# GpSimd instead of VectorE computes the low weight half of one chunk in front of each of four layer norms

## The chip, the cores and the metric

The kernel runs on one core of a Trainium2 chip. The metric is device time in microseconds of one execution; lower is better. Engines are called PE (TensorE, with its weight loads as PEld), DVE (VectorE), ACT (ScalarE), POOL (GpSimd) and SP (SyncE).

## What is computed

A stack of four transformer-like layers on 256 tokens of width 1024, in float32. The part that matters here is the first two layers, each with two residual steps that end in a layer norm:

```python
def layer_norm(x, g, b):
    mu = jnp.mean(xf, axis=-1, keepdims=True)
    var = jnp.mean(jnp.square(xf - mu), axis=-1, keepdims=True)
    y = (xf - mu) * lax.rsqrt(var + LN_EPS) * g + b
...
for i in range(DEPTH):                      # DEPTH = 2
    mix = s5_mixer(h, ...) if i % 2 == 0 else stick_breaking_mixer(h, ...)
    h = layer_norm(ALPHA * h + mix, ln_mix_g[i], ln_mix_b[i])
    h = layer_norm(ALPHA * h + swiglu_ffn(h, w_gu[i], w_down[i]), ln_ffn_g[i], ln_ffn_b[i])
```

Behind them come two hybrid layers (attention, mLSTM, feed-forward) with RMS norms, which the change does not touch.

## The kernel before

**Weights in chunks.** All matrix products run as one sequence of weight chunks of 128 x 2048 float32 elements (1 MB), numbered through all layers. A chunk `c` lives in slot `c % 3` of three buffers: `raw` (as loaded), `w_hi` and `w_lo`. SP loads `raw` (two transfers of 512 KB, `load_chunk`, L390). ACT rounds it to a high part (`split_hi`, L395, counts `hi_done`). DVE computes the low part `w_lo = raw - w_hi` (`split_lo`, L400, counts `lo_done`). PE then makes three products of 128x128 weights with 128x256 activations for each of a chunk's 16 blocks: high by high (L419), high by low (L420), low by high (L421), or two wider ones (L429, L430) in some matrices. Both counts are plain counters of chunks: `lo_done >= c + 1` means that chunks 0 to `c` are split (`weights_split`), and so chunks must be counted in order. SP waits for `lo_done >= j - 2` before it loads chunk `j` into its slot.

**Look-ahead of three.** When PE has finished chunk `i`, ACT and DVE split chunk `i + 3` into the slot that has come free. In the matrices whose results are added to the residual (`evac == "resid"`) this is done by `resid_hi` on ACT (it waits for `chunk_done` of the chunk) and `resid_lo` on DVE.

**Order around a layer norm.** Every engine's order is written out by hand. There are four layer norms, n = 0 to 3, behind the matrices `ssm_out` (4 chunks), `down0` (11), `sb_out` (4) and `down1` (11). DVE's list for such a matrix is `resid_vector`: it adds the product tiles to the residual, prepares centred tiles `xn` and their squares, and calls `resid_lo` for the chunks. With 4 chunks the last two `resid_lo` (indices 2 and 3) stand together in front of the layer norm; with 11 chunks index 10 stands there. Then comes `layer_norm_vector`:

- L1124: the variance, from a PSUM row and `rstd` in SBUF. It waits for ACT's square and copy of the mean (`norm_scale`, L886 and L887). ACT then takes logarithm and exponential (L891, L894) to give `rstd`.
- `centre(q)` (L1129: `xn - dm_sb`) and `scale(q)` (L1134: `xn * rstd`) for four pairs of tiles; each has both inputs in SBUF. `centre` is followed by a wait of DVE for itself.
- ACT makes the normed tiles `res` and, for the first half, `x_hi` (`normed_pair`, L919, L928, L897); DVE makes `x_lo` (`low`, L1150, or L1119 for n = 3) and the second half of `x_hi`.
- `split(0)`, `split(1)`: DVE's `w_lo` of the next two chunks, whose `w_hi` ACT makes behind its normed tiles (`early_columns`).
- `normalised`, `early_gated`: corrections of the two early chunks, see next.

**What PE does meanwhile.** Behind the last residual chunk PE multiplies the first two chunks of the next matrix with the not yet normed values (`early_tensor`); the mean and scale are corrected afterwards by DVE (L1162, L1168) and ACT (L949, L953). These two chunks are 96 products. Then PE needs `x_lo` of the normed values (`xl_done`, pair by pair in its first chunk) and, for this third chunk, its weights: its number is `c = g.c0 + g.n - 1 + 3`, where `g` is the residual matrix. It is the chunk whose `w_lo` DVE computes last in front of the layer norm. For n = 1 and n = 3 the next users of the corrected early chunks are PE's attention scores (L1324) and the product at L2363.

**POOL.** GpSimd works only at the start (`s5_pool`, L2042 to L2113): tables for the state-space mixer, and the `w_lo` of chunk 0 (L2113), the same operation as L400.

Of the kernel before, what the change touches and what calls it, by code (L numbers as in the profile page):

```python
# [15 lines left out]
F32 = mybir.dt.float32  # L16
# [4 lines left out]
ALU = mybir.AluOpType  # L21
# [11 lines left out]
RING = 3  # L33
# [106 lines left out]
RESIDS = ("ssm_out", "down0", "sb_out", "down1", None, "out0", "ff2_0", "out1", "ff2_1")  # L140
# [106 lines left out]
def stack(nc, w, out):  # L247

    gemms, n_chunks = plan(w)
    G = {g.name: g for g in gemms}  # L250
    ctx = ExitStack()
    with ctx:
# [19 lines left out]
        raw = [sb(f"raw{s}", [P, CH], "raw", 4 * CH * s) for s in range(RING)]  # L272
# [63 lines left out]
        hi_done, lo_done = S("hi_done"), S("lo_done")  # L336
# [60 lines left out]
        def split_lo(dve, c, idx, k):  # L397
            s = (c + k) % RING
            dve.wait_ge(hi_done, idx + (c + 1))
            nc.vector.tensor_tensor(w_lo[s][:, :], raw[s][:, :], w_hi[s][:, :].bitcast(F32), ALU.subtract).then_inc(lo_done, 1)  # L400
# [357 lines left out]
        def early_chunks(n):  # L758

            return {0: ((G["gu0"], 0), (G["gu0"], 1)), 1: ((G["q0"], 0), (G["k0"], 0)), 2: ((G["gu1"], 0), (G["gu1"], 1)),  # L760
                    3: ((G["kv_0"], 0), (G["qa0_0"], 0))}[n]

        def x_index(n):

            return n + 1 if n < 3 else n
# [356 lines left out]
        def layer_norm_vector(dve, g, n):  # L1122
            dve.wait_ge(rstd_done, 3 * n + 2)
            nc.vector.tensor_tensor(rstd[:, :], PS[:, 3, T:2 * T], rstd[:, :], ALU.subtract).then_inc(v_done, 1)  # L1124
            twice = [t[:, :].unsqueeze(1).to_broadcast([P, 2, T]) for t in (dm_sb, rstd)]

            def centre(q):
                pair = xn[:, 2 * q:2 * q + 2, :]
                nc.vector.tensor_tensor(pair, pair, twice[0], ALU.subtract).then_inc(dve_step, 1)  # L1129
                dve.wait_ge(dve_step, v_count.one())  # L1130

            def scale(q):
                pair = xn[:, 2 * q:2 * q + 2, :]
                nc.vector.tensor_tensor(pair, pair, twice[1], ALU.mult).then_inc(scaled, 1)  # L1134

            def high(q):
                dve.wait_ge(res_normed, KT * n + 2 * q + 2)
                if n == 3:
                    for t in (2 * q, 2 * q + 1):
                        nc.vector.tensor_scalar(x_hi[:, t, :], res[:, t, :], gain(4, t), None, ALU.mult).then_inc(xh_done, 1)  # L1140
                    return
                nc.vector.tensor_copy(x_hi[:, 2 * q:2 * q + 2, :], res[:, 2 * q:2 * q + 2, :]).then_inc(xh_done, 2)

            def low(q):
                if n == 3:
                    gained_lo(dve, 4, 2 * q)
                    gained_lo(dve, 4, 2 * q + 1)
                    return
                dve.wait_ge(xh_done, KT * x_index(n) + 2 * q + 2)
                nc.vector.tensor_tensor(x_lo[:, 2 * q:2 * q + 2, :], res[:, 2 * q:2 * q + 2, :],  # L1150
                                        x_hi[:, 2 * q:2 * q + 2, :].bitcast(F32), ALU.subtract).then_inc(xl_done, 2)

            def split(slot):
                e, idx = early_chunks(n)[slot]
                split_lo(dve, e.c0 + RING, idx, idx)

            def normalised(slot):

                e, idx = early_chunks(n)[slot]
                dve.wait_ge(cols_copied, 2 * n + slot + 1)  # L1160
                for m in range(2):
                    ins = nc.vector.scalar_tensor_tensor(out=early[:, slot, m * T:(m + 1) * T], in0=dm_sb[:, :],  # L1162
                                                         scalar=col_sums[:, 2 * slot + m, 0:1],
                                                         in1=early_banks(slot)[:, m, 0:T], op0=ALU.mult, op1=ALU.add)
                ins.then_inc(dve_step, 1)
                dve.wait_ge(dve_step, v_count.one())
                both = early[:, slot, :].rearrange("p (a t) -> p a t", a=2)
                nc.vector.tensor_tensor(both, both, twice[1], ALU.mult).then_inc(early_done, 1)  # L1168

            centre(0)  # L1170
            dve.wait_ge(rstd_done, 3 * n + 3)
            scale(0)
            for q in range(1, 3):
                centre(q)
                scale(q)
            low(0)
            centre(3)
            scale(3)
            low(1)
            high(2)  # L1180
            low(2)
            high(3)
            low(3)
            split(0)
            split(1)
            if n == 3:
                square_sums(dve, 4, 0, 4)
            normalised(0)
            normalised(1)
            if n in (0, 2):  # L1190
                early_gated(dve, n, 0)
                early_gated(dve, n, 1)

        def early_gated(dve, n, slot):
            g, idx = early_chunks(n)[slot]
            z = idx + g.gated0 + 1
            dve.wait_ge(sig_done, z)
            dve.wait_ge(hid_done, idx + g.hid0)
            nc.vector.scalar_tensor_tensor(out=prod[:, 0:T], in0=early[:, slot, 0:T], scalar=col_sums[:, 2 * slot, 1:2],
                                           in1=early[:, slot, T:2 * T], op0=ALU.add, op1=ALU.mult).then_inc(z_done, 1)  # L1200
            dve.wait_ge(z_done, z)
            nc.vector.tensor_copy(hid_hi[:, idx, :], prod[:, 0:T]).then_inc(gated_hi, 1)
            dve.wait_ge(gated_hi, z)
            nc.vector.tensor_tensor(hid_lo[:, idx, :], prod[:, 0:T], hid_hi[:, idx, :].bitcast(F32),
                                    ALU.subtract).then_inc(hid_done, 1)
# [35 lines left out]
        def resid_vector(dve, g, n):  # L1241
            last = g.n - 1
            held = 2 if g.shape == "kt8" else last
            if g.half:
                half_vector(dve, g, n)
                return
            raw_columns(dve, n)
            if n == 3:
                gate_weights(dve)
            for idx in range(g.n):  # L1250
                for t in range(KT):
                    if g.ends[t][0] != idx:
                        continue
                    if n < 4 and t == 4:
                        shifted_tiles(dve, g, n)
                    if n < 4 and t >= 4:
                        shifted_tile(dve, g, n, t)
                    else:
                        add_tile(dve, g, t)
                    if n < 4 and t == 3:  # L1260
                        dve.wait_ge(resid_done, g.resid0 + 4)
                        shift_sum(dve, n)
                        raw_columns_lo(dve, g, n)
                    if n < 4 and t == 5:
                        pair_shift(dve, n)
                    if n in (1, 3) and t == 7:
                        fold_mean(dve, n, 7)
                    if n < 4 and t >= 4:
                        raw_tile_lo(dve, n, 2 * t - 8)
                        raw_tile_lo(dve, n, 2 * t - 7)  # L1270
                    if n == 6:
                        gained_lo(dve, n, t)
                        if t == 5:
                            square_sums(dve, n, 0, 2)
                        if t == 7:
                            square_sums(dve, n, 2, 4)
                    if n < 4 and t == 5:
                        add_squares(dve, n, 0)
                    if n < 4 and t == 6:
                        square_sums(dve, n, 1, 3)  # L1280
                        fold_mean(dve, n, 6)
                    if n in (0, 2) and t == 7:
                        fold_square(dve, n, 6)
                    if n in (1, 3) and t == 7:
                        fold_square(dve, n, 6)
                        fold_square(dve, n, 7)
                if n >= 4 or idx < held:
                    resid_lo(dve, g, idx)
            if n < 4:
                for idx in range(held, g.n):  # L1290
                    resid_lo(dve, g, idx)
            if n < 4:
                layer_norm_vector(dve, g, n)
# [1769 lines left out]
        @block.gpsimd  # L3063
        def _(pool):
            s5_pool(pool)

        @block.tensor
        def _(pe):
# [73 lines left out]
```

## Time and profile before

| | |
|---|---|
| median of 3 runs | 1345.09 us (1344.32 to 1345.76) |
| the profiled execution's own time | 1345.14 us |
| its span in the profile | 1343.3 us |
| granted clock of TensorE | 1.0 |
| PE busy, PEld busy | 98%, 93% of the span |
| DVE, ACT, POOL busy | 70%, 50%, 4% |
| `w_lo` on DVE (L400) | 207 instructions, 2.29 us each |
| `w_hi` on ACT (L395) | 207 instructions, 1.9 us each |
| a load of 512 KB, from issue to landing | median 4.5 to 5.1 us by tensor (5.1 for `ffn_w_gu`) |

PE is busy nearly all the time, but its loads and products overlap, so its share says little about small gaps. A stall shows in the starts of the weight loads instead: in a stretch without stalls they follow each other every 0.12 us.

### The profile page before, as it was taken

The page shows a single profiled execution, that of the slowest core. Times are in us where ns is not written, and L with a number is a line of the kernel's source. Part 1 is how long each engine was busy: PE and PEld are TensorE (multiplying, and loading weights), DVE is VectorE, ACT ScalarE, POOL GpSimd, SP SyncE. Part 2 cuts the span into 40 slices and gives each one's busy share as a digit, 9 for nine tenths or more (in the row PEclk, how much of TensorE's full clock was granted, in tenths as well). Part 3 has the DMA queues.
Part 4 walks back from the last instruction along what each step waited for, and adds up shares of the span by engine and source line. Part 5 has one row for each costly group of instructions (what it writes and reads, how often), then busy time and mean ns, then how long its engine had stood idle before and what let it go on. Part 6 is the DMA issues. An engine that isn't in the chain of part 4 may idle for free.

```text
span 1343.3 us, 25869 instructions
## 1 busy us (share of the span) xinstructions
PE 1314.0 (98%) x10699; PEld 1245.2 (93%) x10699; DVE 944.0 (70%) x1340; ACT 676.2 (50%) x838; POOL 56.7 (4%) x31
## 2 busy tenths in 40 slices
PE   5899999999999999999999999999999999999999
PEld 4599999988999999998989999998898999999988
DVE  8966976657865986657897788775457867877542
ACT  5774643334765653344666545444445554544332
POOL 6910000000000000000000000000000000000000
PEclk9999999999999999999999999999999999999999
DMA  8676486675443576666444456567664535556662
GB/s 157 158 185 185 133 221 184 188 190 180 145 148 96 157 208 185 187 188 176 153 137 147 155 159 217 189 184 192 188 188 127 157 123 192 189 188 187 188 188 63
DMA packets 342809, 227.81 MB, mean 170 GB/s; under 512 B 22616, under 2 KB 337792, under 8 KB 342592
## 3 DMA queue, kind: packets, MB, share of 16 engines
q1 hardware_dynamic: 341200, 226.33, 58.5%
q8 instruction: 67, 1.10, 0.3%
q10 hardware_dynamic: 1520, 0.20, 0.1%
q14 instruction: 22, 0.18, 0.0%
HBM read 224.40 MB, written 1.05 MB: 168 GB/s over the span
## 4 chain that ended last, share of the span: by engine, by line
PE 86%; DVE 7%; ACT 4%; issue 1%; POOL 1%; SPq 0%; DMA 0%; DVEq 0%; ACTq 0%; POOLq 0%
PE PS L419 20%; PE PS L420 20%; PE PS L421 20%; PE PS L429 12%; PE PS L430 6%; DVE w_lo L400 2%; ACT w_hi L395 1%; PE PS L1340 1%; DVE xn L1134 1%; DVE xn L1129 1%; DMA c_rows<-in_ssm_c_re_dram 0%; PE PS L1742 0%; PE PS L2430 0%; PE PS L1324 0%; DVE raw_lo L1089 0%
## 5 line engine op out<-in xcount | busy, mean ns | idle before, releaser
L400 DVE TENSOR_TENSOR w_lo<-raw,w_hi 128x2048 fp32r<-128x2048 f32 x207 | 473.6, 2291 | 144.1 <-ACT w_hi L395 143.3
L419 PE MATMUL PS<-x_hi,w_hi 128*128 128x256 f32 x1792 | 504.1, 281 | 1.0 <-DVE w_lo L400 0.5
L420 PE MATMUL PS<-x_lo,w_hi 128*128 128x256 f32 x1792 | 503.7, 281 | 0.0
L421 PE MATMUL PS<-x_hi,w_lo 128*128 128x256 f32 x1792 | 503.3, 281 | 0.0
L395 ACT ACTIVATE w_hi<-raw 128x2048 fp32r<-128x2048 f32 x207 | 396.4, 1915 | 203.2 <-PE PS L430 139.1
L419 PEld LDWEIGHTS PS<-x_hi,w_hi 128*128 128x128 f32 x1792 | 338.3, 189 | 6.0 <-issue 2.9
L420 PEld LDWEIGHTS PS<-x_lo,w_hi 128*128 128x128 f32 x1792 | 336.6, 188 | 0.1
L421 PEld LDWEIGHTS PS<-x_hi,w_lo 128*128 128x128 f32 x1792 | 336.6, 188 | 0.0
L429 PE MATMUL PS<-hid_both,w_hi 128*128 128x512 f32 x756 | 264.8, 394 | 0.0
L430 PE MATMUL PS<-hid_both,w_lo 128*128 128x256 f32 x756 | 211.8, 280 | 0.0
L429 PEld LDWEIGHTS PS<-hid_both,w_hi 128*128 128x128 f32 x756 | 142.1, 188 | 31.4
L430 PEld LDWEIGHTS PS<-hid_both,w_lo 128*128 128x128 f32 x756 | 142.4, 188 | 0.1
L420 PE MATMUL PS<-hid_both,w_hi 128*128 128x256 f32 x492 | 138.3, 281 | 0.0
L421 PE MATMUL PS<-hid_both,w_lo 128*128 128x256 f32 x492 | 138.2, 281 | 0.0
L419 PE MATMUL PS<-hid_both,w_hi 128*128 128x256 f32 x492 | 137.8, 280 | 0.0
L419 PEld LDWEIGHTS PS<-hid_both,w_hi 128*128 128x128 f32 x492 | 92.9, 189 | 0.9 <-issue 0.7
L420 PEld LDWEIGHTS PS<-hid_both,w_hi 128*128 128x128 f32 x492 | 92.4, 188 | 0.1
L421 PEld LDWEIGHTS PS<-hid_both,w_lo 128*128 128x128 f32 x492 | 92.4, 188 | 0.0
L616 ACT ACTIVATE gate_sb<-PS 128x256 f32<-128x256 f32 x48 | 18.4, 383 | 139.5 <-PE PS L421 138.2
L619 ACT ACTIVATE gate_sb<-gate_sb 128x512 f32<-128x512 f32 x32 | 20.2, 632 | 96.0 <-DVE gate_sb L672 96.0
L659 DVE TENSOR_TENSOR prod<-PS,gate_sb 128x256 f32<-128x256 f32 x48 | 20.3, 424 | 58.6 <-ACT gate_sb L616 58.6
L704 DVE SCALAR_TENSOR_TENSOR res<-res,PS 128x256 f32<-128x256 f32 x48 | 19.7, 419 | 35.5 <-PE PS L430 20.0
(395 smaller groups left out, 1482.1 us busy)
## 6 DMA issues: line engine op xcount, KB each, us to landing
raw<-in_w_ff_dram SPq DMA_DIRECT2D x128, 512.0 KB, 4.5
raw<-in_ffn_w_gu_dram SPq DMA_DIRECT2D x88, 512.0 KB, 5.1
raw<-in_w_in_dram SPq DMA_DIRECT2D x68, 512.0 KB, 4.6
raw<-in_sb_w_qkv_dram SPq DMA_DIRECT2D x24, 512.0 KB, 4.5
raw<-in_ffn_w_down_dram SPq DMA_DIRECT2D x20, 512.0 KB, 4.5
raw<-in_ssm_w_glu_dram SPq DMA_DIRECT2D x16, 512.0 KB, 5.6
raw<-in_w_out_dram SPq DMA_DIRECT2D x16, 512.0 KB, 4.6
raw<-in_ssm_w_out_dram SPq DMA_DIRECT2D x8, 512.0 KB, 4.5
```

The source lines that it names most:

```text
L395: nc.scalar.activation(w_hi[s][:, :], raw[s][:, :], ACT.Copy).then_inc(hi_done, 1)
L400: nc.vector.tensor_tensor(w_lo[s][:, :], raw[s][:, :], w_hi[s][:, :].bitcast(F32), ALU.subtract).then_inc(lo_done, 1)
L419: nc.tensor.matmul(dst, lhs_hi, r_hi, start=start, stop=False, skip_group_check=True)
L420: nc.tensor.matmul(dst, lhs_hi, r_lo, start=False, stop=False, skip_group_check=True)
L421: return nc.tensor.matmul(dst, lhs_lo, r_hi, start=False, stop=stop, skip_group_check=True)
L429: nc.tensor.matmul(PS[:, bank, :], lhs_hi, both.rearrange("p i t -> p (i t)"), start=start, stop=False, skip_group_check=True)
L430: return nc.tensor.matmul(PS[:, bank, 0:T], lhs_lo, both[:, 0, :], start=False, stop=stop, skip_group_check=True)
L616: nc.scalar.activation(gate_sb[:, k, 0:T], PS[:, bank, T:2 * T], g.func).then_inc(sig_done, 1)
L619: nc.scalar.activation(gate_sb[:, k, :], gate_sb[:, k, :], ACT.Square).then_inc(u_done, 1)
L659: nc.vector.tensor_tensor(prod[:, 0:T], PS[:, bank, 0:T], gate_sb[:, k, 0:T], ALU.mult).then_inc(z_done, 1)
L704: ins = nc.vector.scalar_tensor_tensor(out=res[:, t, :], in0=res[:, t, :], scalar=g.alpha, in1=PS[:, tile_bank(g, t), 0:T], op0=ALU.mult, ...
L1129: nc.vector.tensor_tensor(pair, pair, twice[0], ALU.subtract).then_inc(dve_step, 1)
```

## The change

GpSimd takes over one `w_lo` in front of each of the four layer norms: chunk `c = g.c0 + g.n + 2`. It waits until chunks 0 to `c - 1` are counted (`lo_done`) and until ACT has made `w_hi` of chunk `c`. DVE leaves this one out (`last` is `g.n - 1`) and goes on to `layer_norm_vector`. In `split`, DVE now waits for the count of all earlier chunks before it computes the next `w_lo`, so that it is not counted ahead of GpSimd's. ACT, PE and SP keep their lists.

```diff
             def split(slot):
                 e, idx = early_chunks(n)[slot]
+                dve.wait_ge(lo_done, e.c0 + RING + idx)
                 split_lo(dve, e.c0 + RING, idx, idx)
...
+        def norm_low(pool, g):
+
+            c = g.c0 + g.n - 1 + RING
+            pool.wait_ge(lo_done, c)
+            pool.wait_ge(hi_done, c + 1)
+            nc.gpsimd.tensor_tensor(w_lo[c % RING][:, :], raw[c % RING][:, :], w_hi[c % RING][:, :].bitcast(F32),
+                                    ALU.subtract).then_inc(lo_done, 1)
...
             if n < 4:
-                for idx in range(held, g.n):
+                for idx in range(held, last):
                     resid_lo(dve, g, idx)
...
         def _(pool):
             s5_pool(pool)
+            for g in gemms:
+                if g.evac == "resid" and RESIDS.index(g.name) < 4:
+                    norm_low(pool, g)
```

## Rows read from the trace of the kernel before

**Rows 1.** The page, busy time by engine
```profile
PE 1314.0 (98%) x10699; PEld 1245.2 (93%) x10699; DVE 944.0 (70%) x1340; ACT 676.2 (50%) x838; POOL 56.7 (4%) x31
```
**Rows 2.** Waits of the weight loads: us in total, times, longest us
```profile
PEld PS L419 <- DVE w_lo L400: 1.6, 4, 0.5
...
PEld PS L419 <- DVE x_lo L1150: 0.8, 2, 0.4
```
**Rows 3.** Timeline of DVE, first norm: start us, us, engine, line [idle before]
```profile
148.60 2.29 DVE L400 TENSOR_TENSOR w_lo<-raw,w_hi 128x2048 fp32r<-128x2048 f32 x1
150.80 0.42 DVE L1124 TENSOR_TENSOR rstd<-PS,rstd 128x256 f32<-128x256 f32 x1
151.14 0.68 DVE L1129 TENSOR_TENSOR xn<-xn,dm_sb 128x512 f32<-128x512 f32 x1
152.32 0.69 DVE L1134 TENSOR_TENSOR xn<-xn,rstd 128x512 f32<-128x512 f32 x1 [0.50 <-ACT rstd L894]
...
160.69 4.49 DVE L400 TENSOR_TENSOR w_lo<-raw,w_hi 128x2048 fp32r<-128x2048 f32 x2 [0.21 <-ACT w_hi L395]
```
**Rows 4.** Timeline of ACT, first norm
```profile
145.72 1.90 ACT L395 ACTIVATE w_hi<-raw 128x2048 fp32r<-128x2048 f32 x1
...
148.31 0.38 ACT L887 ACTIVATE dm_sb<-PS 128x256 f32<-128x256 f32 x1
...
151.80 0.42 ACT L894 ACTIVATE rstd<-rstd 128x256 f32<-128x256 f32 x1
```
**Rows 5.** Timeline of the weight loads, the two stalls behind the first norm
```profile
158.25 0.19 PEld L419 LDWEIGHTS PS<-x_hi,w_hi 128*128 128x128 f32 x1 [0.39 <-DVE x_lo L1150]
...
163.03 0.19 PEld L419 LDWEIGHTS PS<-x_hi,w_hi 128*128 128x128 f32 x1 [0.46 <-DVE w_lo L400]
```
**Rows 6.** POOL's groups by form: busy us, mean ns, idle before
```profile
L2113 POOL TENSOR_TENSOR w_lo<-raw,w_hi 128x2048 fp32r<-128x2048 f32 x1 | 4.6, 4569 | 3.0 <-PE PS L1814 3.0
```
**Rows 7.** Timelines of DVE, ACT and the weight loads, second norm
```profile
337.00 2.29 DVE L400 TENSOR_TENSOR w_lo<-raw,w_hi 128x2048 fp32r<-128x2048 f32 x1 [0.72 <-ACT w_hi L395]
...
340.72 0.69 DVE L1134 TENSOR_TENSOR xn<-xn,rstd 128x512 f32<-128x512 f32 x1 [0.50 <-ACT rstd L894]
...
338.58 0.38 ACT L887 ACTIVATE dm_sb<-PS 128x256 f32<-128x256 f32 x1
...
357.60 0.19 PEld L1324 LDWEIGHTS PS<-qkv 64*128 64x128 f32 x2 [0.33 <-ACT qkv L953]
```
**Rows 8.** Timelines of DVE and the weight loads, third and fourth norm
```profile
455.58 2.29 DVE L400 TENSOR_TENSOR w_lo<-raw,w_hi 128x2048 fp32r<-128x2048 f32 x1
...
461.50 0.69 DVE L1134 TENSOR_TENSOR xn<-xn,rstd 128x512 f32<-128x512 f32 x1 [0.50 <-ACT rstd L894]
...
646.16 2.29 DVE L400 TENSOR_TENSOR w_lo<-raw,w_hi 128x2048 fp32r<-128x2048 f32 x1 [0.72 <-ACT w_hi L395]
...
649.89 0.69 DVE L1134 TENSOR_TENSOR xn<-xn,rstd 128x512 f32<-128x512 f32 x1 [0.50 <-ACT rstd L894]
...
670.65 0.16 PEld L2363 LDWEIGHTS PS<-res,w_if 128*32 128x32 f32 x8 [0.61 <-ACT rstd L894]
```
**Rows 9.** Timelines of POOL and DVE in the first 17 us, where both work
```profile
10.10 0.63 POOL L2057 TENSOR_TENSOR tb<-tb 128x128 f32<-128x128 f32 x1
...
11.60 0.46 POOL L2064 TENSOR_TENSOR tb<-tb 128x128 f32<-128x128 f32 x1
12.15 1.28 POOL L2068 TENSOR_SCALAR tb<-tb,const 128x64 f32<-128x64 f32 x1
15.36 0.72 POOL L2070 TENSOR_TENSOR d_diag<-d_diag,const 128x256 f32<-128x256 f32 x1 [1.93 <-DMA d_diag<-in_ssm_d_dram]
...
10.34 0.67 DVE L2166 TENSOR_TENSOR tmp_pow<-pow_t 128x256 f32<-128x256 f32 x1
...
11.70 0.90 DVE L2164 TENSOR_TENSOR tmp_pow<-pow_t 128x512 f32<-128x512 f32 x1
...
15.17 1.22 DVE L2183 TENSOR_TENSOR tmp<-PS,tb 128x1024 f32<-128x1024 f32 x1
```

## The prediction

> **What bounds the kernel now.** I read the page's busy times first: PE is busy 98% of the span and POOL 4%, all of that at the start [rows 1]. So the time is the length of PE's list plus its stalls, and an engine beside it matters only where PE waits for it. The second view is the waits of the weight loads: PE waits for DVE's `w_lo` four times (1.6 us in total) and for its `x_lo` twice (0.8 us) [rows 2]. Those are small sums, but they tell where nothing is spare. The third view is the timeline around each of the four layer norms. DVE is there occupied without a break: `w_lo`, then L1124, L1129, L1134 and so on, until the next two `w_lo` [rows 3]. PE covers this time with the two early chunks, and the cover is just too short. At the first norm it stands at 158.25 until DVE's second `x_lo` is done and at 163.03 until its next `w_lo` is done [rows 5]. Loads follow each other every 0.12 us, so with the last loads at 157.68 and 162.39 the true stalls are 0.45 and 0.52 us. At the second norm the stall is at 357.60 (0.33 us, behind DVE's corrected early tile), at the fourth at 670.65 (0.61 us) [rows 7, 8]. **In all four, the last thing that PE waited for comes out of DVE's unbroken chain that begins with the layer norm.** Whatever moves the start of that chain later moves PE by the same; what moves it earlier gives back only these stalls.
>
> **Part by part.**
>
> Removed from DVE: four `w_lo` of 2.29 us. At the first norm DVE did one from 148.60 to 150.89 and L1124 behind it [rows 3]. ACT had finished L887, for which L1124 waits, at 148.31 + 0.38 = 148.69 [rows 4]. So L1124 can now start at 148.75, which is 2.05 us earlier; the third norm has the same shape. At the second, L887 ends at 338.96 and L1124 started with the end of `w_lo` (337.00 + 2.29 = 339.29, with 0.1 us of overlap) [rows 7]: only some 0.16 us are to be had, and at the fourth the same.
>
> Added on POOL: the same subtraction. The one row of this operation on POOL has 4.57 us [rows 6], with nothing on DVE that reads two SBUF tensors beside it. It starts when the `w_lo` before it is counted and `w_hi` is there. First norm: `w_hi` ends at 147.62 [rows 4], the earlier `w_lo` at 148.69, so POOL works from 148.75 to 153.32. Second: 337.00 to 341.57. Third: 455.58 + 2.29 = 457.87, so 457.93 to 462.50. Fourth: 646.16 to 650.73 [rows 7, 8]. PE needs this chunk behind 96 early products, at about 156.4 in the first norm (48 loads of 0.12 us and the stall of 0.45 before 162.5), so it comes 3 us in time. SP's next load into the slot waits for this count and goes 2.4 us later; the chunk it brings is split only when PE has finished the third chunk, 9 us later, against 5.1 us for the transfer (the table above). Both cost nothing, and would cost only if POOL took over 7.5 us.
>
> Moved by it: what DVE does beside POOL. L1124 has one input in PSUM; L1129 and L1134 have both in SBUF. **The trace of the start shows what then happens** [rows 9]. L2164 has 512 elements, for which DVE takes 0.68 [rows 3]; at 11.70 it took 0.90 and ended at 12.60, which is 0.54 us behind the end of POOL's L2064 (12.06), and 512 elements in 0.54 us are DVE's full rate. L2166 (256 elements, 0.42 as L1124) took 0.67 and ended 0.28 us behind POOL's L2057 (10.73). There are seven such pairs between 5 and 12 us in which POOL's instruction began first, and in each the DVE instruction with two SBUF inputs ends as if its data only began to flow when POOL's instruction ended. The other way round, POOL's L2068 took 1.28 us for 64 elements, beside two such DVE instructions, while L2070 took 0.72 for 256. L2183, with one input in PSUM, took 1.22 beside POOL's L2070: no delay. So I take it that the two exclude each other for a whole instruction. Those POOL instructions last up to 0.46 us, mine 4.57 us; this is the unknown of the case, with its ends at "not blocked" and "blocked to the end of POOL". I take the second, because all the nearest rows show it whole.
>
> The Trainium skill, "SBUF — State Buffer", section "SBUF: two separate sides", says the same of any length: GpSimd and a DVE instruction with two SBUF inputs share a port pair, whoever starts first holds it for the whole instruction, and the other fully blocks. The rows above agree for short instructions; no row of this trace shows a long one. This page's rule speaks against the change.
>
> The sum. `centre(0)` (L1129) is issued at about 149.2, when POOL is in its work, and ends 0.54 us behind it:
> - First norm: 153.32 + 0.54 = 153.86; L1134 follows at 153.91 instead of 152.32: **+1.6 us**. The logarithm and exponential, which ended at 152.22 [rows 4], are long there.
> - Third norm: 462.50 + 0.58 = 463.08 instead of 461.50: **+1.6**.
> - Second: 341.57 + 0.58 = 342.15 instead of 340.72: **+1.4**. Fourth: 651.31 instead of 649.89: **+1.4** [rows 7, 8].
> - From there the chain is as before and POOL is idle, so the shift is carried in full to PE's stalls.
>
> Added wait in `split`: for slot 0 POOL has long counted. For slot 1 DVE waits for its own `w_lo` just before. Without a wait two of them take 4.49 us, 0.09 less than twice 2.29 [rows 3]: the overlap is lost, **0.1 us**, which reaches PE at the second and fourth norm, where it waits for what stands behind both, and not at the others. What is queued behind this wait on DVE are the corrections of the early chunks, counted here. What could hold it off altogether is POOL being later than 160.69, 7 us late.
>
> Sum: 1.6 + 1.5 + 1.6 + 1.5 = 6.2 us against the profiled execution's own 1345.14, which is 0.05 from the median of 1345.09: **1351.3 us**.
>
> **The rivals.**
>
> *B, no blocking by a long instruction (the other side: not slower).* Its place is L1129 at 149.2 in the first and third norm. If it takes 0.68 there, the chain is 2.05 us early and PE's stalls of 0.45 and 0.52 vanish: 1.0 us each, and hardly 0.1 in sum at the other two. 1345.1 - 2.1 = **1343.0**. For it: DVE and POOL are separate engines and POOL's code may let go between parts of a long tensor. Against it: every one of the seven pairs. It decides where L1129 starts before POOL ends less 2 us. It can't give more, since the stalls are all there is to give back.
>
> *C, they take turns in parts.* Each DVE instruction with two SBUF inputs then loses some 0.25 us, as at 10.34 [rows 9]. About five fall into POOL's 4.57 us: 1.25 us. First and third norm: 2.05 - 1.25 = 0.8 early, saves 0.8 each; second and fourth: 1.25 + 0.1 - 0.16, 1.2 late each. 1345.1 + 0.8 = **1345.9**.
>
> *D, L1124 is blocked too*, through its SBUF input, or POOL starts so late that it is L1134 that is caught. Then the logarithm and exponential stand behind POOL as well. First norm: L1124 ends at 153.32 + 0.27 = 153.59 instead of 151.22, +2.4; second: 341.84 instead of 339.63, +2.2, and 0.1 for the wait. 2.4 + 2.3 + 2.4 + 2.3 = 9.4: **1354.5**. For it: the input is in SBUF. Against: L2183 [rows 9] with the same order of inputs.
>
> **How the numbers follow.** The forecast (whole blocking of L1129) gets 0.76, D 0.07, C 0.10, B 0.07. Some 0.2% (2.7 us) is what a measurement of this kernel can tell from no change: "same" runs from 1342.4 to 1347.8. The forecast and D are slower: 0.83. B and C lie within: 0.16 with their upper halves. Faster than 1342.4 leaves 0.01, as no case gives it. The forecast's own range is 1349.5 to 1352.8 (POOL's start and end by 0.2 us at each norm, and a stall that was not pinned). The range of 8 in 10 takes in D on top: 1348.0 to 1354.6; B and C are left out with 0.17.
>
> **What would show it.** In the changed profile: L400 has 203 instructions; POOL has four of about 4.57 us, at about 148.8, 338.6, 461 and 651 (each norm moved by those before). In each norm one L1129 of four is long or starts late: in the first it ends 0.54 us behind POOL and lasts some 4.7 us if it is recorded from its issue. L1124 stays at 0.42 us (D: it is the long one). PE's stall at the second `x_lo` grows from 0.45 to about 2 us, part of it at the first `x_lo`; the stall before the fourth chunk stays near 0.5. At the second norm the stalls sum to about 1.9. The granted clock stays 1.0. The prediction is wrong if L1129 keeps 0.68 us while POOL works; if POOL's instruction is much longer than 4.6 us, being itself held up; or if PE's shift at a norm is less than DVE's, which would mean that a stall was not pinned to this chain.

## The result and the profile after

The changed kernel takes 1352.66 us (median of 6 runs, 1351.53 to 1352.90) against 1345.49 (6 runs) for the one before: ratio 1.0052, 95% interval 1.0043 to 1.0062, so 7.2 us slower. The prediction had 1351.3 (1348.0 to 1354.6). The profiled execution took 1352.86 us, its span is 1351.1, the granted clock 0.998.

The page of the changed kernel, busy time by engine, answers to [rows 1]:

```profile
PE 1319.1 (98%) x10699; PEld 1247.3 (92%) x10699; DVE 948.3 (70%) x1336; ACT 676.2 (50%) x838; POOL 75.1 (6%) x35
```

DVE lost four instructions of 2.29 us (9.2 us) and yet is busy 4.3 us more. POOL has four more, 18.4 us. Where DVE's time went is seen in the groups by form:

```profile
L1129 DVE TENSOR_TENSOR xn<-xn,dm_sb 128x512 f32<-128x512 f32 x16 | 23.5, 1468 | 0.0
L1134 DVE TENSOR_TENSOR xn<-xn,rstd 128x512 f32<-128x512 f32 x16 | 11.1, 692 | 0.6
```

Sixteen L1129 take 23.5 us; they would take 10.9 at 0.68 each. The timelines of DVE and POOL at the first and the second norm show which ones are long (compare [rows 3, 7]):

```profile
146.60 2.29 DVE L400 TENSOR_TENSOR w_lo<-raw,w_hi 128x2048 fp32r<-128x2048 f32 x1
148.93 0.42 DVE L1124 TENSOR_TENSOR rstd<-PS,rstd 128x256 f32<-128x256 f32 x1
149.27 4.86 DVE L1129 TENSOR_TENSOR xn<-xn,dm_sb 128x512 f32<-128x512 f32 x1
154.17 0.69 DVE L1134 TENSOR_TENSOR xn<-xn,rstd 128x512 f32<-128x512 f32 x1
...
341.26 0.42 DVE L1124 TENSOR_TENSOR rstd<-PS,rstd 128x256 f32<-128x256 f32 x1 [2.79 <-ACT dm_sb L887]
341.60 2.78 DVE L1129 TENSOR_TENSOR xn<-xn,dm_sb 128x512 f32<-128x512 f32 x1
344.41 0.69 DVE L1134 TENSOR_TENSOR xn<-xn,rstd 128x512 f32<-128x512 f32 x1
```
```profile
148.97 4.61 POOL L1200 TENSOR_TENSOR w_lo<-raw,w_hi 128x2048 fp32r<-128x2048 f32 x1 [75.97 <-DVE w_lo L400]
339.24 4.59 POOL L1200 TENSOR_TENSOR w_lo<-raw,w_hi 128x2048 fp32r<-128x2048 f32 x1 [185.65 <-ACT w_hi L395]
```

POOL ends at 153.58 and L1129 at 154.13, 0.55 behind it; at the second norm 343.83 and 344.38, again 0.55. L1124, with one input in PSUM, stays at 0.42 beside POOL. The third norm is as the first, the fourth as the second (L1129 of 4.86 and 2.78 us). The weight loads answer to [rows 5, 7, 8]:

```profile
158.24 0.19 PEld L419 LDWEIGHTS PS<-x_hi,w_hi 128*128 128x128 f32 x1 [1.61 <-issue]
160.10 0.19 PEld L419 LDWEIGHTS PS<-x_hi,w_hi 128*128 128x128 f32 x1 [0.39 <-DVE x_lo L1150]
164.95 0.19 PEld L419 LDWEIGHTS PS<-x_hi,w_hi 128*128 128x128 f32 x1 [0.54 <-DVE w_lo L400]
176.63 0.19 PEld L419 LDWEIGHTS PS<-x_hi,w_hi 128*128 128x128 f32 x1 [0.31 <-issue]
...
361.48 0.19 PEld L1333 LDWEIGHTS PS<-qkv 64*128 64x128 f32 x2 [0.56 <-ACT qkv L953]
...
678.16 0.16 PEld L2372 LDWEIGHTS PS<-res,w_if 128*32 128x32 f32 x8 [0.74 <-ACT rstd L894]
```

The new stall is the first: 1.61 us in front of the first product that needs `x_lo` (its last pieces come at 158.13). The view labels it "issue", since it could not tell the releaser; the time of the L1150 before it tells it. The last row of the first norm is a stall that I had missed. Before the change the same load stood at 174.58; the rows show it with DVE's third `w_lo` behind the norm, then that `w_lo` after the change:

```profile
174.58 0.19 PEld L419 LDWEIGHTS PS<-x_hi,w_hi 128*128 128x128 f32 x1 [0.16 <-issue]
```
```profile
172.16 2.29 DVE L400 TENSOR_TENSOR w_lo<-raw,w_hi 128x2048 fp32r<-128x2048 f32 x1
```
```profile
174.21 2.29 DVE L400 TENSOR_TENSOR w_lo<-raw,w_hi 128x2048 fp32r<-128x2048 f32 x1
```

The load stands 0.13 us behind the end of this `w_lo` both times (174.45 and 176.50), so the stall labelled "issue" is a wait for the sixth chunk's low half.

All 10699 loads stand in the same order in both traces, so each can be set against its like. What a norm costs is the shift of PE behind it less the shift with which DVE or ACT came into it: first norm 2.05 (the load at 174.58, now 176.63) less 0.21 (DVE's `w_lo` at 146.39, now 146.60) = 1.84; second 3.88 - 2.20 = 1.68; third 5.72 - 3.88 = 1.84; fourth 7.51 - 5.87 = 1.64. Sum 7.0 of the 7.8 by which the spans differ. The rest is 0.2 of the start and some 0.6 in single steps of 0.05 to 0.25 between and behind the norms, which I can't lay to the change. (The shifts of 5.72 and 7.51 are those of the loads at 483.76 and 670.65 in the trace before; 2.20, 3.88 and 5.87 those of ACT's `w_hi`, DVE's `w_lo` and ACT's `w_hi` ahead of the norms.)

### The profile page after: what moved, and what is told of

It is laid out like the page before. It is cut to its first block, busy times and chain, and to the rows that moved or that the text cites. A ratio compares the mean times of both kernels' runs of the same rounds, so it can differ in the third digit from the quotient of the medians.

```text
span 1351.1 us, 25881 instructions
## 1 busy us (share of the span) xinstructions
PE 1319.1 (98%) x10699; PEld 1247.3 (92%) x10699; DVE 948.3 (70%) x1336; ACT 676.2 (50%) x838; POOL 75.1 (6%) x35
## 4 chain that ended last, share of the span: by engine, by line
PE 89%; DVE 6%; ACT 3%; issue 1%; POOL 1%; DMA 0%; SPq 0%; DVEq 0%; ACTq 0%; POOLq 0%
PE PS L419 21%; PE PS L420 21%; PE PS L421 20%; PE PS L429 12%; PE PS L430 6%; DVE xn L1129 2%; DVE w_lo L400 1%; ACT w_hi L395 1%; PE PS L1349 1%; DVE xn L1134 1%; PE PS L1751 0%; PE PS L2439 0%; PE PS L1333 0%; PE PS L2450 0%; PE PS L1361 0%
## 5 line engine op out<-in xcount | busy, mean ns | idle before, releaser
L400 DVE TENSOR_TENSOR w_lo<-raw,w_hi 128x2048 fp32r<-128x2048 f32 x203 | 465.0, 2291 | 143.3 <-ACT w_hi L395 142.1
L1200 POOL TENSOR_TENSOR w_lo<-raw,w_hi 128x2048 fp32r<-128x2048 f32 x4 | 18.4, 4602 | 565.3 <-ACT w_hi L395 371.3
```

The costliest lines, as they stand in the source:

```text
L1200: nc.gpsimd.tensor_tensor(w_lo[c % RING][:, :], raw[c % RING][:, :], w_hi[c % RING][:, :].bitcast(F32), ALU.subtract).then_inc(lo_done, 1)
```

## The experiments

A word on reading them: the start of the kernel (the first 75 us, which wait for transfers) differs by up to 3.4 us from one profiled execution to the next, so times inside a norm are compared with the start of the `w_lo` ahead of it, and totals by the medians.

**Almost nothing on GpSimd (tiny).**

```diff
-            nc.gpsimd.tensor_tensor(w_lo[c % RING][:, :], raw[c % RING][:, :], w_hi[c % RING][:, :].bitcast(F32), ...
+            nc.gpsimd.tensor_tensor(w_lo[c % RING][:, 0:16], raw[c % RING][:, 0:16], w_hi[c % RING][:, 0:16].bitcast(F32), ...
```

> The changed kernel, but GpSimd subtracts only the first 16 of the 2048 columns of its chunk; the other low weights are left as they were. Theory (a GpSimd instruction that reads SBUF holds off VectorE's instructions with two SBUF inputs until it ends): L1129 is short again, the layer norm at norms 1 and 3 starts some 2 us earlier than before the change, and only the stalls of PE can be won: 1343.3 us, L1129 at 0.68 us. Rival (a fixed cost of bringing GpSimd in: its wait, its start, the counts): the loss stays, over 1350 us.

Measured: 1342.94 us, ratio to the kernel before 0.9985 (0.9976 to 0.9994). DVE at the first norm:

```profile
146.34 2.29 DVE L400 TENSOR_TENSOR w_lo<-raw,w_hi 128x2048 fp32r<-128x2048 f32 x1
148.67 0.43 DVE L1124 TENSOR_TENSOR rstd<-PS,rstd 128x256 f32<-128x256 f32 x1
149.01 0.68 DVE L1129 TENSOR_TENSOR xn<-xn,dm_sb 128x512 f32<-128x512 f32 x1
150.20 0.69 DVE L1134 TENSOR_TENSOR xn<-xn,rstd 128x512 f32<-128x512 f32 x1 [0.50 <-ACT rstd L894]
```

The first L1134 is 2.1 us earlier than in [rows 3], and between 150 and 180 us no weight load waits any more. The signals, counts and waits are all still there, so they alone do not make the loss of 7 us. And this is the most that taking this chunk off DVE can win: about 2 us (1.8 between the medians), nearly all of it at the first and third norm, where PE gains 1.3 us each.

**Half of it (half).** The same with columns 0 to 1023.

> The changed kernel, but GpSimd subtracts 1024 of the 2048 columns; the other half of these low weights is left as it was. Theory: GpSimd takes 2.37 us instead of 4.6 and ends at about 151.3 in the first norm, L1129 ends 0.54 us behind it at 151.9, 0.6 us before where the old kernel's L1134 began; at norms 2 and 4 L1129 is issued as GpSimd ends. With 0.2 us for the waits at each norm: 1344.7 us. Rival (a loss in proportion to GpSimd's work): half of +7.2, 1349.1 us.

Measured: 1344.44 us, ratio 0.9996 (0.9987 to 1.0005). POOL and DVE at the first norm:

```profile
148.45 2.39 POOL L1200 TENSOR_TENSOR w_lo<-raw,w_hi 128x1024 fp32r<-128x1024 f32 x1 [77.00 <-DVE w_lo L400]
```
```profile
148.75 2.65 DVE L1129 TENSOR_TENSOR xn<-xn,dm_sb 128x512 f32<-128x512 f32 x1
151.43 0.69 DVE L1134 TENSOR_TENSOR xn<-xn,rstd 128x512 f32<-128x512 f32 x1
```

POOL ends at 150.84, L1129 at 151.40: again 0.56 behind. Half of POOL's work costs nothing that can be told from noise (0.3 us under its comparison), the second half 7.5 us: the loss is no rate but an end time, which matters once it lies behind the point where the norm could have gone on.

**GpSimd's whole work, VectorE's operands moved (psum_both).** ACT writes the reciprocal deviation to a free PSUM bank too, and the norm reads both rows from PSUM:

```diff
+        def rstd_bank(n):
+            return (early_chunks(n)[0][0].bank0 + 1) % RING if n < 3 else 2
...
+            if n < 4:
+                nc.scalar.activation(PS[:, rstd_bank(n), 0:T], rstd[:, :], ACT.Exp, scale=-0.5).then_inc(rstd_done, 1)
+                nc.scalar.activation(rstd[:, :], rstd[:, :], ACT.Exp, scale=-0.5).then_inc(act_step, 1)
+                a_count.one()
+                return
...
-                nc.vector.tensor_tensor(pair, pair, twice[0], ALU.subtract) ...
+                nc.vector.tensor_tensor(pair, pair, PS[:, 3, 0:T].unsqueeze(1).to_broadcast([P, 2, T]), ALU.subtract) ...
-                nc.vector.tensor_tensor(pair, pair, twice[1], ALU.mult) ...
+                nc.vector.tensor_tensor(pair, pair, PS[:, rstd_bank(n), 0:T].unsqueeze(1).to_broadcast([P, 2, T]), ALU.mult) ...
```

> The changed kernel with GpSimd's whole 4.6 us, but L1129 reads the mean and L1134 the reciprocal deviation from PSUM (ScalarE writes it there and, in one more instruction, to SBUF), so each has one SBUF input. Theory: neither is held off, both keep 0.68 us while GpSimd works, and the first L1150 (two SBUF inputs) comes after its end: 1343.5 us, under both kernels. Rival (GpSimd and VectorE slow each other down whatever the operands, or the loss comes from the counts and waits): 1350 us or more.

Measured: 1342.98 us, ratio 0.9986 (0.9977 to 0.9995). POOL and DVE (L1137 and L1142 are the old L1129 and L1134):

```profile
149.38 4.63 POOL L1208 TENSOR_TENSOR w_lo<-raw,w_hi 128x2048 fp32r<-128x2048 f32 x1 [77.92 <-DVE w_lo L400]
```
```profile
149.68 0.68 DVE L1137 TENSOR_TENSOR xn<-xn,PS 128x512 f32<-128x512 f32 x1
150.84 0.69 DVE L1142 TENSOR_TENSOR xn<-xn,PS 128x512 f32<-128x512 f32 x1 [0.48 <-ACT PS L898]
151.44 0.68 DVE L1137 TENSOR_TENSOR xn<-xn,PS 128x512 f32<-128x512 f32 x1
152.16 0.69 DVE L1142 TENSOR_TENSOR xn<-xn,PS 128x512 f32<-128x512 f32 x1
152.76 0.68 DVE L1137 TENSOR_TENSOR xn<-xn,PS 128x512 f32<-128x512 f32 x1
153.47 0.69 DVE L1142 TENSOR_TENSOR xn<-xn,PS 128x512 f32<-128x512 f32 x1
154.08 0.68 DVE L1158 TENSOR_TENSOR x_lo<-res,x_hi 128x512 fp32r<-128x512 f32 x1
```

Six DVE instructions begin within POOL's 4.63 us and run at full speed (0.68 to 0.69 us each), and the first with two SBUF inputs is issued at 154.08, just behind POOL's end at 154.01. The work of DVE and POOL is as in the changed kernel (ACT has one short instruction more); only where the second input lies differs. Each kernel against its own comparison, that turns 7.2 us lost into 1.8 won, as much as tiny wins.

The trace of the kernel before had shown this already, in rows that the prediction did not read. While POOL makes the tables at the start, DVE works beside it with one input in PSUM:

```profile
37.01 2.29 DVE L2229 TENSOR_TENSOR s_out<-tab_c,PS 128x2048 f32<-128x2048 f32 x1
37.21 4.58 POOL L2109 TENSOR_TENSOR s_out<-s_out,tmp 128x2048 f32<-128x2048 f32 x1
```

DVE takes the 2.29 us for 2048 elements that L400 takes with POOL idle, and the next three (L2236, L2241, L2236, 1024 elements each), which run beside this POOL instruction and the one behind it (41.87, 3.87 us), take 1.22 to 1.23, as L2278 does at 64.59 with POOL idle.

**The same without GpSimd (psum_before), and psum_both again beside it (psum_both2).** The two PSUM reads and ACT's extra write put into the kernel before.

> The old kernel, VectorE doing all low weights and GpSimd none, with the two PSUM inputs of psum_both (mean and deviation). It tells whether psum_both won by taking 2.3 us off VectorE or by reading PSUM. Theory: reading PSUM alone changes nothing, 1345.2 us. Rival (the PSUM reads, or ScalarE's extra write, are what is faster): 1343 us.

> psum_both once more, on the same chip as psum_before. Theory: 2 us under it, 1343.0 us.

Measured: psum_before 1345.22 us, ratio 1.0000 (0.9991 to 1.0009); psum_both2 1343.34, ratio 0.9986 (0.9977 to 0.9995). So reading PSUM is no gain in itself; the gain of 2 us comes with the `w_lo` of 2.29 us taken off DVE, which the change had meant to have and lost to the blocking.

**Only the mean in PSUM (psum_mean).**

```diff
-                nc.vector.tensor_tensor(pair, pair, twice[0], ALU.subtract) ...
+                nc.vector.tensor_tensor(pair, pair, PS[:, 3, 0:T].unsqueeze(1).to_broadcast([P, 2, T]), ALU.subtract) ...
```

> The changed kernel with the mean alone read from PSUM (L1129), the deviation (L1134) from SBUF as before. Theory: L1129 keeps 0.68 us while GpSimd works, and now L1134 is the one that is held off: it ends 0.54 us behind GpSimd, at about 154.1 in the first norm, where it ended at 154.86. Some 0.7 us saved at each norm of the 7.2: 1349.5 us. Rival (L1129 itself is the sensitive one): like psum_both, 1343.0 us.

Measured: 1349.50 us, ratio 1.0032 (1.0020 to 1.0044). POOL and DVE:

```profile
148.26 4.61 POOL L1200 TENSOR_TENSOR w_lo<-raw,w_hi 128x2048 fp32r<-128x2048 f32 x1 [76.92 <-DVE w_lo L400]
```
```profile
148.56 0.68 DVE L1129 TENSOR_TENSOR xn<-xn,PS 128x512 f32<-128x512 f32 x1
149.74 3.68 DVE L1134 TENSOR_TENSOR xn<-xn,rstd 128x512 f32<-128x512 f32 x1 [0.51 <-ACT rstd L894]
```

The block moved to the next instruction with two SBUF inputs: L1134 ends at 153.42, 0.55 behind POOL's 152.87. The kernel is 4.3 us above its comparison (1345.18) instead of 7.2.

**What GpSimd must do to block (memset, onein).** Each ran once, so they are read for the record of L1129 and not for the total. The first new line is memset's, the second onein's.

```diff
-            nc.gpsimd.tensor_tensor(w_lo[c % RING][:, :], raw[c % RING][:, :], ...
+            nc.gpsimd.memset(w_lo[c % RING][:, :].bitcast(F32), 0.0).then_inc(lo_done, 1)                              # memset
+            nc.gpsimd.tensor_scalar(w_lo[c % RING][:, :], raw[c % RING][:, :], 0.0, None, ALU.mult).then_inc(lo_done, 1)  # onein
```

> GpSimd only writes (a memset of the chunk's w_lo to zero) in place of the subtraction: the low weights of this chunk are zero. If only reads exclude each other, L1129 keeps 0.68 us while the memset runs and the time is that of tiny, 1343 us; if any GpSimd instruction does, L1129 ends 0.54 us behind the memset.

> GpSimd does a tensor_scalar with one SBUF input (raw times zero) in place of the subtraction, 2048 columns: the low weights of this chunk are zero. Open: does a GpSimd instruction with one input hold VectorE off too? If the whole instruction excludes the other, the first L1129 of the norm ends 0.54 us behind its end; if only a two-input one does, L1129 keeps 0.68 us.

The rows of memset, then of onein:

```profile
151.31 1.81 POOL L1200 MEMSET w_lo<- 128x2048 f32 x1 [77.76 <-DVE w_lo L400]
```
```profile
151.63 0.68 DVE L1129 TENSOR_TENSOR xn<-xn,dm_sb 128x512 f32<-128x512 f32 x1
```
```profile
149.48 5.38 POOL L1200 TENSOR_SCALAR w_lo<-raw 128x2048 fp32r<-128x2048 f32 x1 [77.81 <-DVE w_lo L400]
```
```profile
149.76 3.90 DVE L1129 TENSOR_TENSOR xn<-xn,dm_sb 128x512 f32<-128x512 f32 x1
```

The memset, which only writes, blocks nothing here: L1129 takes 0.68 within its 1.81. With one input POOL blocks too, but neither of my two expectations fits: L1129 ended at 153.66, so its data began to flow at 153.11, 3.6 us behind POOL's start and 1.75 us ahead of its recorded end (154.86). The three later norms show the same 3.6 us from POOL's start. So for this form the block is not the whole recorded instruction. Its total, also a single run, is 1349.51 us against 1345.18. The total of memset, 1345.72 us in a single run, can't be set against the 1343 I expected: in that execution the `w_lo` ahead of the first norm began 2.5 us later than in [rows 3]'s execution (148.95 against 146.39), and behind the fourth norm its loads were only 0.36 late, so the norms gave back 2.2, near the 2.4 of tiny's trace.

**The two waits alone (waits).** The kernel before with this line only:

```diff
                 e, idx = early_chunks(n)[slot]
+                dve.wait_ge(lo_done, e.c0 + RING + idx)
                 split_lo(dve, e.c0 + RING, idx, idx)
```

> The old kernel, VectorE doing all low weights, with nothing but the two added waits in split. My sum had 0.1 us at norms 2 and 4 alone: 1345.7 us. The trace of the changed kernel suggests 0.2 us at every norm (0.07 at slot 0 and 0.13 at slot 1, both reaching PE): 1346.3 us.

Measured: 1346.47 us, ratio 1.0011 (1.0002 to 1.0020), 1.7 above the 1344.74 of its comparison; in the traces the spans differ by 1.1. DVE's two `w_lo` behind the first norm:

```profile
160.82 4.62 DVE L400 TENSOR_TENSOR w_lo<-raw,w_hi 128x2048 fp32r<-128x2048 f32 x2 [0.29 <-ACT w_hi L395]
```

They take 4.62 us where the kernel before had 4.49 (0.13 for slot 1), and the idle time ahead of them is 0.29 where it was 0.21 (0.07 for slot 0). At the fourth norm ACT's `w_hi` is done 0.2 us earlier, and the first of the two `w_lo` starts right behind the DVE instruction ahead of it, with the added wait (659.69) as without it (658.70); slot 0 costs nothing there. Behind the second to the fourth norm the shift of PE grew by 0.18, 0.18 and 0.13, near the 0.2 expected; behind the first by 0.55, of which some 0.3 is a pause of DVE at 170.10 that the changed kernel does not have. The waits cost more than the 0.2 us of my sum (0.3 to 2.7 us by the interval), and they reach PE at every norm.

**Filling the wait for the exponential (hoist).** The kernel before, with one line moved:

```diff
             centre(0)
+            centre(1)
             dve.wait_ge(rstd_done, 3 * n + 3)
             scale(0)
-            for q in range(1, 3):
-                centre(q)
-                scale(q)
+            scale(1)
+            centre(2)
+            scale(2)
             low(0)
```

> The old kernel (GpSimd not used) with centre(1) moved in front of scale(0), so that VectorE fills the 0.5 us in which it waits for ScalarE's exponential. Theory (PE is pinned to VectorE's chain in front of these stalls): the chain is some 0.5 us early at each norm, up to the size of the stalls: 1345.1 - 4 x 0.45 = 1343.3 us. Rival (the stalls hang on something else): 1345 us, no change.

Measured: 1345.69 us, ratio 1.0003 (0.9994 to 1.0012): no change, the expectation fell. ACT and the weight loads of hoist:

```profile
152.94 1.09 ACT L919 ACTIVATE res<-xn,vec 128x256 f32<-128x256 f32 x2 [1.09 <-DVE xn L1134]
...
158.45 1.92 ACT L395 ACTIVATE w_hi<-raw 128x2048 fp32r<-128x2048 f32 x1
```
```profile
162.75 0.19 PEld L419 LDWEIGHTS PS<-x_hi,w_hi 128*128 128x128 f32 x1 [0.90 <-DVE w_lo L400]
```

The `w_lo` ahead began 0.36 us earlier than in [rows 3]'s execution (146.03 against 146.39), so 0.36 is to be added. The stall at the second `x_lo` is gone, but the one before the fourth chunk grew from 0.46 to 0.90: that load stands at 162.75 + 0.36 = 163.11, against 163.03. It waits for a `w_lo` which waits for `w_hi`, and that one stands on ACT behind eight normed tiles, which begin with the first `scale`. `centre(1)` ahead of it made the first `scale` 0.26 us later (152.22 + 0.36 against 152.32), and `w_hi` ended 0.07 later. So the stall before the fourth chunk hangs on ACT's list from the first `scale` on, and not on how tightly DVE's list is packed.

## Why the prediction was right, and where it was off

- **The mechanism** (whole blocking of L1129): right. 0.55 us behind POOL's end at both norms shown, against the 0.54 taken from the short pairs [rows 9]. tiny, half, psum_mean and psum_both show that it is POOL's end time and the place of the second input that decide; beside them only the added waits have a cost. Rival B (1343.0) fell, and the price it was given turned out to be that of tiny and psum_both. C fell with the 4.86 us of L1129, D with the 0.42 us of L1124.
- **What the Trainium skill says** ("SBUF — State Buffer", "SBUF: two separate sides": the port pair is held for the whole instruction) holds here for a two-input instruction of 4.6 us, which was the open point; memset agrees with its remark that the block is against a GpSimd operation that reads SBUF. For the one-input `tensor_scalar` the trace differs: 3.6 of 5.4 us. The measurement decides.
- **Readings of [rows 9] that were off.** "Those POOL instructions last up to 0.46 us": L2057 in the same rows has 0.63. And beside the seven pairs there is an eighth in which POOL began first, with a one-input `tensor_scalar`: POOL's L2051 ran from 8.93 to 9.32, DVE's L2166 (128 elements, two SBUF inputs) was issued at 8.99 and ended at 9.32 too, with 0.32 us against the 0.29 of the L2164 before it. Held to POOL's end, it would have ended 0.15 behind it, as L2168 (11.04, 0.29 us, 128 elements) did behind L2059. So this form had not held DVE to its end there either, as onein then showed at length.
- **The shift of the norm.** Forecast 1.6, 1.4, 1.6, 1.4. Measured at the first L1134, less the shift of the `w_lo` (or `w_hi`) ahead: 154.17 - 152.32 - 0.21 = 1.64; 344.41 - 340.72 - 2.20 = 1.49; 467.02 - 461.50 - 3.88 = 1.64; 657.26 - 649.89 - 5.87 = 1.50. The small excess is POOL's: it took 4.6 us, not 4.57, and at the second norm it began 0.14 us behind `w_hi` (339.10), where I had 0.1.
- **The step that failed** is the added wait: "0.1 us, which reaches PE at the second and fourth norm ... and not at the others". It is 0.07 for slot 0 at the first three norms and 0.13 for slot 1, and it reaches PE at all four: at the first and third norm through the stall at 174.58, where PE waits for the sixth chunk's `w_lo`. The view labels that stall "issue", and I had read only labelled waits. PE's shifts exceed those of the first L1134 by 0.20, 0.19, 0.20 and 0.14: 0.7 us where the sum had 0.2.
- **The sum.** Forecast 6.2; measured in the norms 7.0, between the medians 7.2. The waits (+0.5) and POOL's length and start (+0.3) make up for it. The time itself came out 1.4 above the forecast, near the upper end of its own range (1352.8): 0.8 from the norms, 0.4 because the kernel before has a median of 1345.49 over six runs, the rest not resolved.
- **PE's place.** Forecast: the stall at the second `x_lo` grows to about 2 us, part of it at the first; it was 1.61 at the first and 0.39 at the second, as before. The stall before the fourth chunk stayed (0.54). The second norm's were forecast at 1.9 in sum; they are labelled 0.33, 0.39, 0.53 and 0.56, 1.8 in sum.
- **POOL's lateness cost nothing**, as said: no load waits for its chunk, and SP's later transfer shows nowhere.
- **A reason too broad.** "The last thing that PE waited for comes out of DVE's unbroken chain" is true as far as a shift of the chain's start goes, but hoist shows that one of these stalls hangs on ACT, whose list starts with the same chain. The 0.21 us in which L400 waits for ACT's `w_hi` stand in [rows 3]. For an earlier start it made no difference; for a tighter order on DVE it did.

## What to carry to other kernels

Before work is given to GpSimd beside VectorE, look at where each VectorE instruction of that stretch has its inputs: here those with two in SBUF stood still until a GpSimd `tensor_tensor` was done (and for 3.6 of the 5.4 us of a `tensor_scalar`), those with one in PSUM ran on. A single SBUF input is not shown to be safe in the same way: in the kernel before, DVE's L2132 (a `tensor_scalar` of 64 elements, issued at 6.25 while POOL's L2048 ran until 6.54) took 0.33 us, where L2141 of the same form took 0.20. So either put the shared operand in PSUM (here 2 us won instead of 7.2 lost, with nearly the same work) or size GpSimd's part so that it ends before the first two-SBUF instruction that matters (here half of it cost nothing). And a stall that the profile lays to "issue" must be looked into before a small cost is called hidden.

## What was not expected of the hardware

- GpSimd's `tensor_scalar` with one input took 5.4 us for 128x2048 elements, longer than the two-input subtraction (4.6), and held VectorE for 3.6 us of it. What it does in the rest was not tried.
- A wait of VectorE on its own last count cost 0.13 us between two long instructions (4.62 against 4.49 us for the pair). A wait that has long been met cost 0.07 us in front of a `w_lo` that was itself waiting for ACT's `w_hi` (it began 0.10 instead of 0.03 us behind the end of `w_hi`), and nothing at the fourth norm, where the `w_lo` had no such wait.
